# Residuals seeded into PSUM by ScalarE instead of added by identity matmuls, with the norm made in token layout

## The reference

```
ALPHA = (2 * DEPTH) ** 0.25                          # DEPTH = 2
for l in range(2):                                   # first block
    h = x @ w_in[l]                                  # q, k, v of three attentions, gates
    merged = g0 * (o_a @ w_a) + g1 * (o_b @ w_b) + g2 * (o_c @ w_c)
    x = layer_norm(ALPHA * x + merged @ w_out[l], ln1_g[l], ln1_b[l])
    u_gate, u_up = split(x @ w_ffn_in[l])
    x = layer_norm(ALPHA * x + (silu(u_gate) * u_up) @ w_ffn_out[l], ln2_g[l], ln2_b[l])
for l in range(2):                                   # second block
    x = layer_norm(ALPHA * x + 0.5 * swiglu(x, ffn1...), ln1_g, ln1_b)
    y = concat(conv, gmlp, sparse attention)(x @ w_in)
    x = layer_norm(ALPHA * x + y @ w_out, ln2_g, ln2_b)
    x = layer_norm(ALPHA * x + 0.5 * swiglu(x, ffn2...), ln3_g, ln3_b)
```

## Time and profile before

| | |
|---|---|
| three runs | 2027.08, 2028.13, 2028.14 us; median 2028.13 |
| profiled execution, first to last instruction (span) | 2026.5 us |
| its own time | not given apart from the span; the runs' median is 1.6 us longer |
| TensorE busy | 2010.1 us, 99% |
| VectorE busy | 1274.6 us, 63% |
| ScalarE busy | 927.4 us, 46% |
| GpSimd busy | 32.2 us, 2% |
| read from HBM | 349.36 MB |

### The profile page before, as it was taken

The page is one execution under the profiler, slowest core; times in us unless marked ns, Lnnn a source line. Parts: engine busy times, 40 slices in busy tenths (PEclk is TensorE's granted clock), DMA queues, the critical chain, the costliest instruction groups (busy, mean ns, idle before and its releaser), DMA issues.

```text
span 2026.5 us, 32504 instructions
## 1 busy us (share of the span) xinstructions
PE 2010.1 (99%) x14176; PEld 1838.1 (91%) x14176; DVE 1274.6 (63%) x1844; ACT 927.4 (46%) x1275; POOL 32.2 (2%) x56
## 2 busy tenths in 40 slices
PE   8999999999999999999999999999999999999998
PEld 7888999999887999999999989799999998979997
DVE  6566666555756665655665567765566556776555
ACT  4445444443545444544444454454444445445442
POOL 0000000000000000000000000000000000000000
PEclk9999999999999999999999999999999999999999
DMA  8543555666554556496556646458656664545663
GB/s 287 167 151 132 187 169 170 196 207 190 167 163 138 166 167 186 144 266 187 167 177 189 189 134 167 103 158 252 187 167 187 188 188 133 160 135 158 188 190 101
DMA packets 416133, 352.51 MB, mean 174 GB/s; under 512 B 28816, under 2 KB 361080, under 8 KB 415992
## 3 DMA queue, kind: packets, MB, share of 16 engines
q1 hardware_dynamic: 415992, 350.44, 57.3%
HBM read 349.36 MB, written 1.05 MB: 173 GB/s over the span
## 4 chain that ended last, share of the span: by engine, by line
PE 94%; DVE 3%; ACT 2%; issue 0%; DMA 0%; DVEq 0%; SPq 0%
PE ps L201 29%; PE ps L203 29%; PE ps L202 29%; PE ps L1446 2%; PE ps L1527 2%; PE ps L1565 1%; DVE hl L1990 1%; PE ps L1599 1%; ACT hl L1749 1%; DVE er L2157 0%; DVE small L2116 0%; ACT er L1841 0%; PE ps L1637 0%; DVE er L2114 0%; PE ps L1570 0%
## 5 line engine op out<-in xcount | busy, mean ns | idle before, releaser
L1990 DVE TENSOR_TENSOR hl<-raw,hl 128x1024 fp32r<-128x1024 f32 (+2 forms) x555 | 756.3, 1393 | 393.4 <-ACT hl L1749 392.4
L201 PE MATMUL ps<-xt,hl 128*128 128x256 f32 (+1 forms) x2672 | 753.9, 282 | 0.0
L202 PE MATMUL ps<-xt,hl 128*128 128x256 f32 (+1 forms) x2672 | 746.2, 279 | 0.0
L203 PE MATMUL ps<-xt,hl 128*128 128x256 f32 (+1 forms) x2672 | 745.9, 279 | 0.0
L1749 ACT ACTIVATE hl<-raw 128x2048 fp32r<-128x2048 f32 (+1 forms) x323 | 613.2, 1900 | 182.8 <-PE ps L203 169.5
L201 PEld LDWEIGHTS ps<-xt,hl 128*128 128x128 f32 (+1 forms) x2672 | 501.0, 187 | 4.6 <-issue 1.5
L202 PEld LDWEIGHTS ps<-xt,hl 128*128 128x128 f32 (+1 forms) x2672 | 501.1, 188 | 3.1
L203 PEld LDWEIGHTS ps<-xt,hl 128*128 128x128 f32 (+1 forms) x2672 | 500.8, 187 | 0.2
L201 PE MATMUL ps<-hl,o 128*128 128x512 f32 x656 | 261.5, 399 | 0.0
L203 PE MATMUL ps<-hl,o 128*128 128x512 f32 x656 | 259.0, 395 | 0.0
L202 PE MATMUL ps<-hl,o 128*128 128x512 f32 x656 | 258.8, 394 | 0.0
(11 more groups left out here) (202 smaller groups left out, 1606.5 us busy)
## 6 DMA issues: line engine op xcount, KB each, us to landing
raw<-in_w_in SPq DMA_DIRECT2D x83, 1024.0 KB, 5.1
raw<-in_w_ffn_in SPq DMA_DIRECT2D x88, 512.0 KB, 5.1
raw<-in_ffn_gate SPq DMA_DIRECT2D x88, 512.0 KB, 4.1
raw<-in_ffn_up SPq DMA_DIRECT2D x88, 512.0 KB, 5.3
raw<-in_ffn_down SPq DMA_DIRECT2D x44, 1024.0 KB, 5.1
raw<-in_w_ffn_out SPq DMA_DIRECT2D x22, 1024.0 KB, 5.0
raw<-in_w_out SPq DMA_DIRECT2D x12, 1024.0 KB, 5.1
raw<-in_w_branch_a SPq DMA_DIRECT2D x8, 1024.0 KB, 4.9
```

What stands on the lines that cost most here:

```text
L201: e.matmul(out, l[0], r[0], start=start, stop=False)
L202: e.matmul(out, l[0], r[1], start=False, stop=False)
L203: return e.matmul(out, l[1], r[0], start=False, stop=stop)
L1990: e.tensor_tensor(lo[:, c], m["raw"][:, k % NRAW, 0:n][:, c], hi[:, c].bitcast(F), ALU.subtract).then_inc(s.low.up(("low", k), *([("low", ...
```

## The change

- `residual`, the identity `ai` and the 320 matmuls go. In their place stands the step `seed`: ScalarE copies `X[:, i, c*512:(c+1)*512]` into the bank before the first matmul of its sum, and all matmuls of the sum are issued without the start flag (`mm3_onto`), so that they add to what is there. There are 40 seeds, four for each norm: `acc_pair` takes two banks and seeds them. In an FFN the pair for `i` = 0 comes after the first two hidden units and the pair for `i` = 1 after the third; in the output projections two pairs, one for each `c`, come before the first matmuls.
- `X` must then be the real x. `ln_norm` now does what `ln_last` did: VectorE takes `(sum - mean) * g` from the two banks, then `* rstd + b`, both over 512 columns, four instructions for each half of the tokens; ScalarE has no part in it. Transposing x gives `XT` directly, so `ln_affine` goes, and `ln_split` makes the high part from PSUM in two instructions of 512 columns (ScalarE) and the low part in four of 256 (VectorE).
- Gain and bias are needed as rows on all partitions. `rows_in` loads them before each norm, four loads of 256 KB (2 KB to each of 128 partitions), into four buffers of the ring `ET` (in the second block's middle norm: two of `RT` and a part of `sg`). The 20 small loads of gains and biases by channel go, and `last_in` with its two 512 KB loads.
- A seeded bank must have been written as a whole by an ordinary group of matmuls before. `Ring` keeps for each bank whether its last use was such a group (`dense`), `take(True)` gives only such banks and `take(False)` prefers the others. Groups that fill a bank in two halves now set the start flag once for the bank.
- `in_halves` has one form: half of the second unit's pieces (twelve matmuls of 256 columns, or six of 512) always stand ahead of `turn()`.

```
-    def take(self):
-        slot = self.order.pop(0)
+        self.dense, self.spare = [False] * len(aps), None
+
+    def take(self, dense=None):
+
+        dense = self.spare if dense is None else dense
+        like = [x for x in self.order if dense is None or self.dense[x] == dense]
+        slot = like[0] if like or dense else self.order[0]
+        self.order.remove(slot)
...
+def mm3_onto(e, out, l, r):
+
+    e.matmul(out, l[0], r[0], start=False, stop=True, skip_group_check=True)
+    e.matmul(out, l[0], r[1], start=False, stop=True, skip_group_check=True)
+    return e.matmul(out, l[1], r[0], start=False, stop=True, skip_group_check=True)
...
-    def in_halves(pieces, more=None):
-        turn, affine = P.half
+    def in_halves(pieces):
+        turn, split = P.half
         P.half = None
         pieces(0, 0, (0, 1))
...
+        pieces(1, 0, (0,))
+        turn()
+        pieces(1, 0, (1,))
+        split()
...
     def layer_norm(acc, tail, final=False):
...
+        stats(0)
         if final:
-            add("ln_last", 0, acc[0], smalls[0], new, ("x turned", v, 0))
             for t in tail:
                 t()
-            rest()
-            add("ln_last", 1, acc[1], smalls[1], new, ("x turned", v, 1))
+            stats(1)
             return
-        stats(0)
         for t in tail[:3]:
             t()
         low = P.prep_next()
         turn(0)
         tail[3]()
-        rest()
-        affine(0, lambda: low(2))
+        low(2)
+        split(0)
         stats(1)
         low(2)
...
+    def seed(b, i, c):
+        dense([b])
+        add("seed", b, i, c, ("xn", P.xv, i, c) if P.xv else ("x", i))
+
+    def acc_pair(i=None, c=None):
+
+        pair = [PB.take(True), PB.take(True)]
+        for n, b in enumerate(pair):
+            seed(b, *((i, n) if c is None else (n, c)))
+        return pair
...
     def ffn(...)
-        for j, b in enumerate(first_units([gate_up(0), gate_up(1)], begin)):
+        for j, b in enumerate(first_units([gate_up(0), gate_up(1)])):
             up(j, b, True)
-        acc.append([PB.take(), PB.take()])
+        acc = [acc_pair(i=0)]
         up(2)
+        acc.append(acc_pair(i=1))
         up(3)
+        rows_in(g, b_, row_slots())
...
     def second(l, o, nxt)
             for c in range(2):
                 if c == 0:
                     P.flush()
-                for i in range(2):
-                    acc[i].append(PB.take())
-                yield from residual(acc, c)
+                for i, b in enumerate(acc_pair(c=c)):
+                    acc[i].append(b)
+                PB.spare = None if c else False
                 yield from out_part(I["w_out_2"][l], acc, [[("o1 gmlp", l)], [("o1 conv", l)]], c, ks=(2, 0))
...
 sync_engine
+    def rows_in(srcs, places, v):
+        for src, x in zip(srcs, places):
+            e.wait_ge(*T[x.before])
+        e.wait_ge(*T["rows read", v - 1] if v > 1 else (None, 0))
+        for src, x in zip(srcs, places):
+            e.dma_start(x.ap, src.partition_broadcast(128)).then_inc(s.rows.up(("rows", v)), 16)
...
 tensor_engine
     def n_part(g, b, src, r, k0, i, src_events, first, last, after, seeded=False):
...
+        if seeded:
+            e.wait_ge(*T[b.seed])
...
 scalar_engine
+    def ln_split(i, banks, v):
+        for q, b in enumerate(banks):
+            e.wait_ge(*T[b.full])
+            e.activation(XT[:, 0, 4 * q:4 * q + 4, i * 128:(i + 1) * 128], b.ap.rearrange("p (k t) -> p k t", k=4), ACT.Copy).then_inc(
+                done.up(("xt high", v, i, q)), 1)
+
+    def seed(b, i, c, x_event):
+        e.wait_ge(*T[x_event])
+        e.wait_ge(*T[b.before])
+        e.activation(b.ap, X[:, i, c * 512:(c + 1) * 512], ACT.Copy).then_inc(done.up(b.seed), 1)
...
 vector_engine
+    def ln_norm(i, acc, small, rows, v, out="xn"):
+        mv, rs = small[1:3]
+        e.wait_ge(*T["rows", v])
+        e.wait_ge(*T["x turned", v - 1, i])
+        e.wait_ge(*T["mv", v, i])
         for c in range(2):
+            e.scalar_tensor_tensor(X[:, i, c * 512:(c + 1) * 512], acc[c].ap, mv[:, 0:1], rows[c].ap, ALU.subtract, ALU.mult).then_inc(done.up(acc[c].free), 1)
         e.wait_ge(*T["rs", v, i])
         e.wait_ge(*done.now)
         for c in range(2):
             x = X[:, i, c * 512:(c + 1) * 512]
+            e.scalar_tensor_tensor(x, x, rs, rows[2 + c].ap, ALU.mult, ALU.add).then_inc(
+                done.up((out, v, i, c), *([("rows read", v)] + [r.free for r in rows if r.ring] if i and c else [])), 1)
```

More of the change, by code:

```diff
@@ L520, in proj_t, with first_units @@
         return t_unit(*t_proj(*args, **kw))
-    def first_units(two, more):
+    def first_units(two):
         P.ahead = 1
@@ L576, in layer_norm @@
         tail[3]()
-        rest()
-        affine(0, lambda: low(2))
+        low(2)
+        split(0)
         stats(1)
         low(2)
[L581 to L587, removed]
+        for x in rows:
+            if x.ring is ET:
+                ET.give(x)
+            elif x.ring is RT:
+                RT.give(x)
+        P.half = (lambda: turn(1), lambda: split(1))
+    def seed(b, i, c):
[6 more added lines that the diff above has]
+        return pair
     def out_part(w, acc, src_events, c, r=0, ks=(0, 2)):
@@ L618, in out_end, with ffn @@
         return [lambda c=c, ks=ks: part(c, 1, ks) for c in range(2) for ks in ((0, 1), (2, 3))]
-    def ffn(f, gate_up, down, scale, before, setup=iter(())):
+    def ffn(f, gate_up, down, scale, before, norm, setup=iter(())):
         v = P.xv
+        g, b_ = norm
         def up(j, b=None, n=False):
@@ L1054, in second @@
         acc, tail = swiglu(l, 1, ("ht read", ("first", 1) if l == 0 else ("second", 0, 2), 10))
-        layer_norm(acc, cols[:, 12:28], cols_event, tail)
+        layer_norm(acc, tail)
+        rows_in(I["ln2_g_2"][l], I["ln2_b_2"][l], [RT.take() for _ in range(2)] + [Place(m["sg"][:, 1, c * 512:(c + 1) * 512], ("merge split", 1)) for c in range(2)])
         w_in = I["w_in_2"][l]
@@ L1461, in turn_copy, with n_part @@
         turn(b, blocks, *taken)
[L1463 removed]
+    def n_part(g, b, src, r, k0, i, src_events, first, last, after, seeded=False):
         hi, lo = (x.rearrange("p (k c) -> p k c", k=4) for x in hl(g, UNIT))
@@ L1517, in ln_turn, with out_piece @@
             turn(b, [X[:, i, (4 * q + k) * 128:(4 * q + k + 1) * 128] for k in range(4)], ("x turned", v, i))
-    def residual(b, i, c, events, first, after):
-        if first:
-            e.wait_ge(*T[b.before])
-        e.wait_ge(*T["ai"])
-        for x in events:
-            e.wait_ge(*T[x])
-        for k in range(4):
-            for z in (0, 1):
-                ins = e.matmul(b.ap[:, k * 128:(k + 1) * 128], XT[:, z, 4 * c + k, i * 128:(i + 1) * 128], ai, start=first and k == 0 and z == 0,
-                               stop=not first and k == 3 and z == 1)
-        ins.then_inc(done.up(b.full, *after), 1)
-    def out_piece(g, b, r, i, ks, src_events, last, events):
+    def out_piece(g, b, r, i, ks, src_events, events):
         hi, lo = (x.rearrange("p (k c) -> p k c", k=4) for x in hl(g, UNIT))
```

242 lines of the change are left out of this document (85 added, 157 removed).

## The result

The changed kernel takes **2041.22 us** (median of 4 runs, 2040.18 to 2042.59) against 2028.14 for the kernel before on the same chip (2027.08 to 2028.40): 1.0067 times as long, 95% interval 1.0055 to 1.0079. It is slower by 13.1 us, where 15.1 us less was forecast; the range given ends at 2027. The profiled execution spans 2039.8 us.

The account below looks back on a forecast made before the run. TensorE, busy 2010.1 of 2026.5 us, was taken as the bound. Residual matmuls -34.5, output-projection norms +4.0, FFN norms +4.6, second block's projection +10.8 sum to -15.1 on 2028.13: 2013 us, range 2001 to 2027.

Parts of the forecast that it names:

- I charge nothing: All norms: the 40 row loads, issued a whole FFN or merge ahead into free buffers, were put at no cost.
- The third rival: Row loads starve the weights in their shared queue, 4.2 us at each of 10 norms, giving 2055 us; chance 0.04.
- the sentence against it: Against starved weights: loads are issued three units ahead, and TensorE waited for no weight load but the first.
- The second block's projection, 5.4 a layer net: Output projection: waits of 6.0 us less a 0.6 us wait that goes, 10.8 us in two layers.
- 4.0, 1.0 and 0.8: Waits there, us a layer: first seed behind exponentials and a split; second seed pair; VectorE's turn of compressed scores.
- The norms, 1.0 and 1.1: TensorE's waits, us a norm: 1.0 at four after output projections, 1.1 at five after FFNs.
- The second rival: Every wait is larger, from hand-overs or a low half between in the norms' chain: 2020 to 2032 us; chance 0.20.
- -34.5 us for the residual matmuls: TensorE: removing all 320 saves 34.5 us, 18 times 1.73 plus four times 0.84, 0.108 us per matmul.

Follow-up runs that it names:

- Run 1: The changed kernel, with the row loads of the second block's middle norm requested where attention begins instead of right behind the first norm: 2022.36 us.
- Runs 7 and 8: Run 1's kernel with 24, then 30, throwaway matmuls while TensorE waits for the first seed of the second block's output projection: 2019.99 and 2019.49 us.
- Run 4: Run 1's kernel with VectorE's second low half of the weights moved ahead of the statistics of row half 1 in every norm: 2027.95 us.
- run 10: Run 1's kernel with VectorE making x in one pass instead of two, leaving out mean subtraction and gamma multiplication: 2014.53 us.
- run 5: Run 1's kernel with all 40 seeds made by identity matmuls on TensorE instead of by ScalarE: 2047.32 us.
- kernel 6: Run 1's kernel with only the 8 seeds of the second block's output projection made by identity matmuls on TensorE: 2019.58 us.
- kernel 3: Run 1's kernel with the first seed of the second block's output projection ahead of the exponentials and the other pair also moved earlier: 2017.30 us.

## Why the prediction was wrong

Forecast and measurement lie 28.2 us apart. By the table, 14.7 of it are the first projection, 7.9 the norms, 4.4 the output projection and 1.1 the start of the program.

- **"I charge nothing" for the row loads**: the step that failed most, +14.7 us. It said that each is issued a whole FFN or merge ahead of its norm and that their buffers are free by then. That looked at the bytes and at the buffers. The same step of the diff has a third wait, for the previous norm's rows to have been read, and in the second block the request stands right behind that norm. Run 1 shows it: the wait gone, the time gone, 16.0 us at the two places. The third rival had this effect (weights late behind row loads) with another cause, transfer time, and a chance of 0.04; and the sentence against it, that loads are issued three units ahead, is just what a blocked queue ends.
- **The second block's projection, 5.4 a layer net**: 4.0, 1.0 and 0.8 were right (4.08, 1.02, 0.78) and so was their reason. Missing was what a 4 us hole does to the matmuls behind it (7.6 measured). Runs 7 and 8 show this as a cost of its own, 1.4 to 1.6 us in kernel 1; the two holes in the first projection pay about 2 each.
- **The norms, 1.0 and 1.1**: the passes (1.41 a pair) and the waits of the transposes were sized well. I followed VectorE's list to x and stopped, though the low half for the twelve matmuls behind the transposes stands next on it. Run 4 shows that it and x want the same time on VectorE, and in run 10 TensorE gains exactly what this low half gains: 1.8 to 1.9 us a norm measured. The second rival named "a low half that comes between" with 0.20.
- **-34.5 us for the residual matmuls** was right: run 5 puts them back at 0.11 us each. Seeds outside the second block's output projection cost nothing, as forecast: no FFN and no first-block projection shifts, and a seed takes 0.6 us.
- With the one wait out of the way the change is worth 0.25%, and with the seeds early too, 0.54%, against the 0.75% forecast. The residual matmuls were priced well and the places of the waits named well; what the forecast had at nothing, the wait in the queue above all, turned a gain into a loss.

## What to carry to other kernels

When a change puts a request into a queue that also feeds the critical engine, read every semaphore that the request waits for and ask when it is signalled, not only how many bytes it moves and whether the target is free: what it costs is the time that all requests behind it are held. Follow the in-order engine past the result you are after to the next thing that the critical engine needs from it. And a hole in TensorE can cost more than its length, because the matmuls behind it run at half rate: in the same place, a hole shortened from 4.1 to 1.25 us gave back none of that part, and one of 0.78 all. When an edit takes one instruction out of a chain, look at what that instruction had covered: here a result of GpSimd.

## What the runs showed that I had not expected

- The half rate doesn't begin with the matmuls behind a hole: in kernel 1 TensorE came on at 1284.04 after 4.1 us and started a matmul every 0.23 us for one microsecond before they slowed to 0.43. In the changed kernel they were slow from the first. Nor does the length of a wait decide alone. In the output projection, 1.06 us was followed by a clock of 1.00 three times (both layers of kernel 5, one of kernel 6) and once by 0.50; 1.95 us in kernel 3 was followed by 0.50 in one layer and by 1.00 in the other; 1.2, 1.25, 2.5 and 4.1 us there came with a fall to 0.50 each time. At the norms of kernel 4, eight waits of 1.2 to 1.5 us were all followed by 1.00. The kernel before, whose longest wait behind its start is 0.6 us, keeps 1.00 to its last matmul. These are single executions; on what else it depends stays open.
- The first product matmuls of the program differ in pace between kernels that are alike up to there: from 10 us on they start every 0.43 us until about 14 in the kernel before and past 15 in the changed one, and at full pace almost at once in kernel 1, though the windows print a granted clock of 1.00 in all three. They print 1.00 where the trace has no record of the clock. The first record, of the full clock, stands at 14.2 us in the kernel before, at 16.5 in the changed one and at 8.6 in kernel 1, ahead of its first product matmul, and that is where the full pace begins in each, as it does in the other kernels. So these matmuls too ran at the lower level; why the clock rises sooner in one profile than in another, no run shows. It makes up to 2.6 us from one profile to the next, and it is why differences of 2 us above rest on the starts of matmuls at the place itself.
